# First stage reordered: Fourier tables early, broadcasts late, rows turned before the last modulation unit

## The reference

```python
c_act = silu(c)
mod = c_act @ w_ada + b_ada                    # 1024 x 6144: shift_m, scale_m, gate_m, shift_f, scale_f, gate_f
h = rms_norm(x, g_norm_mix) * (1 + scale_m) + shift_m
p = h @ w_in                                   # 512 + 5*1024 columns: u_f, v, b_g, c_g, ga, gb
y_a = fourier_mix(u_f) @ w_fourier             # a DFT over tokens and over 128 channels of each of 4 groups
y_b = (b_g * conv3(c_g * v)) @ w_conv_out
x = x + gate_m * ((sigmoid(ga) * y_a + sigmoid(gb) * y_b) @ w_o)
# then: 16 experts of width 2048 chosen by the tokens' scores, a second block with two kinds of
# sparse attention, and a third block (two layers) with four kinds of attention and a gated MLP
```

## Time and profile before

| | |
|---|---|
| median of 3 runs | 2204.26 us (2202.93 to 2204.53) |
| the profiled execution | 2204.55 us |
| its span, first to last instruction | 2202.8 us |
| TensorE (PE) busy | 1738.9 us, 79% |
| VectorE busy | 802.5 us, 36% |
| ScalarE busy | 637.9 us, 29% |
| granted TensorE clock, mean | 0.884 of 2.4 GHz |
| transferred | 613.54 MB, mean 279 GB/s |

### The profile page before, as it was taken

One profiled execution on the slowest core, in us unless ns is written; L12 is line 12 of the kernel. 1 busy time (PEld: TensorE's weight loads), 2 busy tenths in 40 slices (PEclk: granted clock), 3 DMA queues, 4 the chain that ended last, 5 costly groups with the idle time before them and its releaser, 6 DMA issues.

```text
span 2202.8 us, 32667 instructions
## 1 busy us (share of the span) xinstructions
PE 1738.9 (79%) x13392; PEld 1261.2 (57%) x13392; DVE 802.5 (36%) x1579; ACT 637.9 (29%) x1128; POOL 79.6 (4%) x133
## 2 busy tenths in 40 slices
PE   6999966565665666656555899879989998999998
PEld 3789921111121221112111799878879987989996
DVE  3364621111101111111100657665655545565553
ACT  2334310000000000000000456635644334654333
POOL 2000010000000000000000200100100000000000
PEclk8999977888878777787878899999989999989999
DMA  9886779999999999999999653316164544145540
GB/s 350 296 286 231 287 286 428 428 429 428 428 428 429 428 428 428 429 429 428 428 428 421 213 192 116 96 68 225 26 224 154 191 164 148 40 154 163 190 167 26
DMA packets 152998, 613.54 MB, mean 279 GB/s; under 512 B 8816, under 2 KB 62138, under 8 KB 128312
## 3 DMA queue, kind: packets, MB, share of 16 engines
q1 hardware_dynamic: 148928, 604.47, 69.7%
q0 software_dynamic: 3200, 7.14, 1.1%
q10 hardware_dynamic: 760, 0.39, 0.1%
HBM read 610.88 MB, written 5.03 MB: 280 GB/s over the span
## 4 chain that ended last, share of the span: by engine, by line
PE 51%; DMA 38%; DVE 5%; issue 3%; ACT 2%; DVEq 1%; POOL 1%; SPq 0%; ACTq 0%; POOLq 0%
PE psum L1393 49%; DMA ring<-in_w_down_e 18%; DMA ring<-in_w_up_e 18%; DVE ring_r L685 2%; PE psum L1475 1%; DMA ring<-in_w_in 1%; DMA x<-in_x 1%; PE psum L1721 1%; ACT arena L1046 0%; DVE arena L2271 0%; ACT ring_r L676 0%; DVEq L2265 0%; POOL stat L924 0%; DVE arena L2405 0%; POOL stat L927 0%
## 5 line engine op out<-in xcount | busy, mean ns | idle before, releaser
L1393 PE MATMUL psum<-ring,arena 128*32 128x512 f32 (+2 forms) x4314 | 534.3, 639 | 281.0 <-DMA ring<-in_w_up_e 129.5
L1393 PE MATMUL psum<-xR_r,ring_r 128*128 128x256 f32 x4416 | 561.4, 287 | 5.4 <-DVE xR_r L1931 3.4
L1393 PEld LDWEIGHTS psum<-xR_r,ring_r 128*128 128x128 f32 x4416 | 540.7, 193 | 16.7 <-issue 9.5
L1393 PEld LDWEIGHTS psum<-ring,arena 128*32 128x32 f32 x4314 | 153.7, 133 | 627.9 <-DMA ring<-in_w_up_e 209.6
L685 DVE TENSOR_TENSOR ring_r<-ring,ring_r 128x1024 fp32r<-128x1024 f32 (+2 forms) x332 | 377.7, 1173 | 255.1 <-ACT ring_r L676 254.7
L676 ACT CAST ring_r<-ring 128x1024 fp32r<-128x1024 f32 (+2 forms) x332 | 319.2, 1006 | 441.3 <-PE psum L1393 421.2
L1393 PE MATMUL psum<-arena 128*128 128x256 f32 (+7 forms) x1270 | 193.6, 387 | 26.4 <-DVE arena L2148 9.9
L2145 DVE TENSOR_TENSOR arena<-arena,psum 128x512 f32<-128x512 f32 x16 | 16.9, 1054 | 474.1 <-PE psum L1393 474.1
L1393 PE MATMUL psum<-ring_r,xR_r 128*128 128x256 f32 (+3 forms) x1344 | 176.5, 289 | 10.6 <-DVE xR_r L1909 6.1
L1393 PEld LDWEIGHTS psum<-ring_r,xR_r 128*128 128x128 f32 x1344 | 166.8, 195 | 14.2 <-issue 5.0
L1393 PE MATMUL psum<-ring_r,arena_r 128*128 128x512 f32 (+1 forms) x912 | 170.6, 349 | 2.1 <-DVE mt L2509 2.1
(11 more groups left out here) (242 smaller groups left out, 941.2 us busy)
## 6 DMA issues: line engine op xcount, KB each, us to landing
ring<-in_w_gate_e SPq DMA_DIRECT2D x64, 2048.0 KB, 25.9
ring<-in_w_down_e SPq DMA_DIRECT2D x63, 2048.0 KB, 26.4
ring<-in_w_up_e SPq DMA_DIRECT2D x62, 2048.0 KB, 24.8
ring<-in_w_in SPq DMA_DIRECT2D x30, 2048.0 KB, 12.3
ring<-in_w_ada SPq DMA_DIRECT2D x12, 2048.0 KB, 9.6
ring<-in_w_gate SPq DMA_DIRECT2D x22, 1024.0 KB, 5.5
ring<-in_w_up SPq DMA_DIRECT2D x22, 1024.0 KB, 8.5
ring<-in_w_down SPq DMA_DIRECT2D x10, 2048.0 KB, 7.8
```

Source lines behind the costliest of these rows:

```text
L1393: return nc.tensor.matmul(o, l, r, start=s, stop=e)
```

## The change

- SyncE asks for the two Fourier tables right behind `win0`, on a semaphore of their own (`in_dft`); the two gate broadcasts come behind `win3`, the router's loads, its bias and `g_final` behind `win5`.
- GpSimd's two replications wait until `uf0` is finished.
- The transposes `n1_0` to `n1_2` come ahead of the first step of `ada1`; `n1_3` comes behind its second step. The numbering of pieces, and with it the banks, changes: `uf0` (piece 8) now shares its bank with `n1_1` (4), `n1_3` (7) with `n1_0` (3).
- ScalarE writes the high part of the modulated rows (one activation with scale and bias, straight out of PSUM), and for `n1_1` and `n1_3` a full copy too; VectorE writes the full copy for `n1_0` and `n1_2`, and the low parts.
- `dfta` comes behind `v0`, `dftb` behind `v1`.
- In all blocks TensorE waits for the first low half of a chunk at a piece's beginning, for the second ahead of the second half of the contraction.

```diff
-PIECES = ([f"ada{u}" for u in ADA_FIRST] + names("n1_", 4) + names("uf", 2) + names("dfta", 4) + names("dftb", 2)
-          + with_ada(names("v", 4) + names("b", 4) + names("c", 4) + names("ga", 4) + names("gb", 4))
+PIECES = ([f"ada{u}" for u in ADA_FIRST[:3]] + names("n1_", 3) + [f"ada{ADA_FIRST[3]}", "n1_3"] + names("uf", 2)
+          + ["v0"] + names("dfta", 4) + with_ada(["v1"]) + names("dftb", 2)
+          + with_ada(names("v", 4)[2:] + names("b", 4) + names("c", 4) + names("ga", 4) + names("gb", 4))
...
+        moved = bT[:, 0:4, :].rearrange("p (a b) t -> p a b t", a=2)
...
                 if i == 0:
+                    sp.dma_start(dfts, a["c_dft"][:, 0:TT * 2 * T].rearrange("p (k n) -> p k n", k=TT)).then_inc(in_dft, 16)
+                    sp.dma_start(dftg, a["c_dft"][:, TT * 2 * T:].rearrange("p (k n) -> p k n", k=2)).then_inc(in_dft, 16)
+                if i == 3:
                     sp.dma_start(gate_m, a["b_ada"][:, 2 * D:3 * D].partition_broadcast(P).squeeze(1)).then_inc(in_b1, 16)
                     sp.dma_start(gate_f, a["b_ada"][:, 5 * D:6 * D].partition_broadcast(P).squeeze(1)).then_inc(in_b1, 16)
-                    sp.dma_start(dfts, a["c_dft"][:, 0:TT * 2 * T].rearrange("p (k n) -> p k n", k=TT)).then_inc(in_b1, 16)
-                    sp.dma_start(dftg, a["c_dft"][:, TT * 2 * T:].rearrange("p (k n) -> p k n", k=2)).then_inc(in_b1, 16)
+                if i == 5:
                     sp.wait_ge(consts_set, 6)
...
             pool.wait_ge(rel_na, 16 * 9)
+            pool.wait_ge(g_ready, AT["uf0"] + 1)
             pool.dma_start(na_rep.rearrange("r (q n) -> r q n", q=GRID_W),
...
+            def high_moved(h):
+
+                i = AT[f"n1_{h}"]
                 piece(act, i)
+                if h == 0:
+                    act.wait_ge(mod_set, 1)
+                if h % 2 == 0:
+                    act.wait_ge(n1_full, h // 2 + 1)
+                for full in (False, True)[:1 + h % 2]:
+                    for m in range(2):
+                        k = 2 * h + m
+                        d = moved[:, h // 2, m, :] if full else xR[:, 0, k, :]
+                        o = nc.scalar.activation(d, G(i)[:, m * T:m * T + T], ACT.Identity, bias=mod[:, k:k + 1],
+                                                 scale=Am[:, k:k + 1])
+                o.then_inc(n1_hi, 1)
+
+            high.half(0, 0)
+            high_moved(0)
+            high.half(0, 1)
+            for h in range(1, 4):
+                high_moved(h)
+            for i in range(2):
+                high.half(1, i)
...
+            def split_half(blk, name, l, i):
                 c = (C1AT, C2AT, C3AT)[blk][name]
-                pe.wait_ge(c_low[blk], (0 if l is None else l * (2 * len(CH3))) + 2 * (c + 1))
-                return chunk(blk, c)[1:]
+                pe.wait_ge(c_low[blk], (0 if l is None else l * (2 * len(CH3))) + (2 * c + i + 1))
+
+            def second_half(k, kt, blk, name, l):
+                if k == kt // 2:
+                    split_half(blk, name, l, 1)
...
             for p, u in enumerate(ADA_FIRST):
+                if p == 3:
+                    pe.wait_ge(n_xn, 1)
+                    for h in range(3):
+                        turn_first(h)
+                    mod_second(ADA_FIRST[2])
                 mod_first(u)
-                if p >= 1:
+                if 1 <= p < 3:
                     mod_second(ADA_FIRST[p - 1])
             mod_second(ADA_FIRST[-1])
+            turn_first(3)
...
+            def low_moved(h):
+                i = AT[f"n1_{h}"]
+                full = moved[:, h // 2, :, :] if h % 2 else temp(h // 2)
+                v.drain()
+                dve.wait_ge(n1_hi, h + 1)
+                v.tensor_tensor(xs[1][:, 2 * h:2 * h + 2, :], full, xs[0][:, 2 * h:2 * h + 2, :].bitcast(F32),
+                                ALU.subtract).then_inc(g_free[i % 4], 1)
...
+            full_moved(0)
+            low.half(0, 0)
+            low_moved(0)
+            low.half(0, 1)
+            full_moved(2)
+            for h in range(1, 4):
+                low_moved(h)
             for i in range(2):
-                low.half(0, i)
-            modulated(AT["n1_0"], Am, mod[:, 0:8])
-            low.ahead(-1)
+                low.half(1, i)
```

More of the change, by code:

```diff
@@ L1102, in _, with taken_rows @@
             high = High(act, 0)
-            high.ahead(-1)
-            for i in (AT["uf0"], AT["uf1"]):
-                high.ahead(C1AT[f"uf{i - AT['uf0']}"])
+            def high_moved(h):
+                i = AT[f"n1_{h}"]
                 piece(act, i)
-                h = i - AT["uf0"]
+                if h == 0:
[16 more added lines that the diff above has]
+                high.half(1, i)
+            def taken_rows(nm, dstT, h):
+                i = AT[f"{nm}{h}"]
+                piece(act, i)
+                nc.scalar.copy(dstT[:, 2 * h:2 * h + 2, :],
+                               G(i).rearrange("p (k t) -> p k t", k=2)).then_inc(g_free[i % 4], 1)
+            for h in range(2):
+                i = AT[f"uf{h}"]
+                piece(act, i)
                 nc.scalar.copy(uf[:, :, 256 * h:256 * h + 256],
                                G(i).rearrange("p (t n) -> p t n", t=TT)).then_inc(g_free[i % 4], 1)
+                high.ahead(C1AT[f"uf{h}"])
+            taken_rows("v", vT, 0)
+            high.ahead(C1AT["v0"])
             for g in range(4):
@@ L1114, in _ @@
             for nm, dstT in (("v", vT), ("b", bT)):
-                for h in range(4):
-                    i = AT[f"{nm}{h}"]
+                for h in range(nm == "v", 4):
                     high.ahead(C1AT[f"{nm}{h}"])
-                    piece(act, i)
-                    nc.scalar.copy(dstT[:, 2 * h:2 * h + 2, :],
-                                   G(i).rearrange("p (k t) -> p k t", k=2)).then_inc(g_free[i % 4], 1)
+                    taken_rows(nm, dstT, h)
                     if f"{nm}{h}" in ADA_AFTER:
@@ L1463, in cols3, with turn_first @@
                 return ready(o, l) if r == count - 1 else o
+            def turn_first(h):
+                i = AT[f"n1_{h}"]
+                bank_free(pe, i)
+                for m in range(2):
+                    for t in range(TT):
+                        k = 2 * h + m
+                        o = nc.tensor.transpose(G(i)[:, m * T + t * P:m * T + t * P + P], xn1[:, t, k * P:k * P + P], ident)
+                o.then_inc(g_ready, 1)
             def turn_x(first, src, l=None, normed=None, at=0):
@@ L1529, in _ @@
             xs = (xR[:, 0], xR[:, 1])
[L1530 to L1531 removed]
             for h in range(2):
[L1533 to L1550 removed]
+                rows3(AT[f"uf{h}"], 0, f"uf{h}", xs, first=[AT[f"n1_{j}"] for j in range(4)] if h == 0 else None)
             prior = None
@@ L1554, in _ @@
                     cols3(AT[f"{nm}{h}"], 0, f"{nm}{h}", xs)
+                    if f"{nm}{h}" == "v0":
+                        taken(pe, AT["uf0"], AT["uf1"])
+                        pe.wait_ge(in_dft, 16 * 2)
+                        for g in range(4):
+                            i = AT[f"dfta{g}"]
+                            bank_free(pe, i)
+                            for k in range(TT):
+                                o = mm(G(i), uf[:, k, g * P:g * P + P], dfts[:, k, :], k == 0, k == 1)
+                            o.then_inc(g_ready, 1)
                     if f"{nm}{h}" in ADA_AFTER:
@@ L1558, in _ @@
                         mod_second(ADA_AFTER[prior])
+                    if f"{nm}{h}" == "v1":
+                        for c_ in range(2):
+                            i = AT[f"dftb{c_}"]
+                            bank_free(pe, i)
+                            for m in range(2):
+                                g = 2 * c_ + m
+                                taken(pe, AT[f"dfta{g}"])
+                                for c in range(2):
+                                    o = mm(G(i)[:, m * T:m * T + T], dftg[:, c, :], Bcs[:, g, c * T:c * T + T], c == 0, c == 1)
+                            o.then_inc(g_ready, 1)
                     prior = f"{nm}{h}"
@@ L2005, in _ @@
                     low.ahead(C1AT[f"{nm}{h}"])
-            dve.wait_ge(in_b1, 16 * 4)
+                    if f"{nm}{h}" == "v1":
+                        for c in range(2):
+                            i = AT[f"dftb{c}"]
+                            piece(dve, i)
+                            parts(pair(G(i)), (fmR[:, 0], fmR[:, 1]), slice(2 * c, 2 * c + 2)).then_inc(g_free[i % 4], 1)
+            dve.wait_ge(in_b1, 16 * 2)
             gate_half(0)
```

57 lines of the change are left out of this document (19 added, 38 removed).

## The result

The changed kernel takes 2190.58 us (median of five, 2186.11 to 2193.42), beside 2204.53 us for the kernel before in the same set. The medians differ by 13.95 us, where 10.1 were forecast (2194.2). The ratio over the single executions is 0.9927 [0.9911, 0.9943], which is 16.1 us. Two further timed sets of both kernels give 0.9937 [0.9924, 0.9950] and 0.9921 [0.9906, 0.9936], and one single time is 2187.9 us; together about 16 us. The direction was right, and so were the places, but for some that were missing. The size was too small by 4 to 6 us.

A forecast was written before the change was run, and what follows sets the result against it. TensorE was taken as the chain from 64.46 us until the experts, which are DMA bound. Stage one -7.2 and half waits -3.0 took 10.2 off 2204.55; with the median 0.3 lower, 2194.2 us, range 2190 to 2199 (8 in 10).

The forecast's parts named there:

- the term of the half waits: All blocks: TensorE starting on a chunk's first half shortens its waits for low halves, -3.0 us, bounds 0 and -5.
- The term of stage one: Ahead of the experts: stall -5.3, Fourier products -2.25, their cut +0.3, together -7.2 us, bounds -4.6 and -8.4.
- The head: Start to end of `uf1`: vectors ready at 39.6 us, `uf0` starts at 45.8, `uf1` ends at 59.2 (58 to 61.5).
- my formula: End of `uf1` is 57.3 + 0.44 h us, h being how long the low clock stays, 3.1 to 4.5 us.
- The stall and the Fourier products: Behind `uf1`: `win1` lands near 42 us, ending the stall, -5.3 us; Fourier products at 2.4 GHz, -2.25, cut in two, +0.3.
- What is moved later: Replications, gate broadcasts and router loads cost nothing; `win3` lands at 79 us, needed at about 89, slack 10 us.
- the signs of being wrong: `uf0` starting after 47 us, a wait for `win3` near 89 us, or layer three as long as before.
- The rival of the collision: Replications collide with `win3`: 21.4 us on its way, landing at 81 us; slower by 0.2% only from 104; chance 0.04.
- the likeliest: Whole kernel: all terms count, 2194.2 us, own range 2191 to 2197; chance 0.55.
- only stage one counts: Rival: half waits only move a wait to the next VectorE result, 2197.1 us; chance 0.2.
- the stall stays: Rival: `win1` still lands after 58 us, set by something other than queue order, 2200 to 2203 us; chance 0.05.
- the head is later: Rival: slower ScalarE-VectorE hand-overs or clock rising only in 7 us, `uf1` ends at 62, 2197 to 2200 us; chance 0.13.

The follow-up runs named there:

- queue_only: The kernel before with the new order of requests alone, replications behind `uf0` included: 2203.56 us, 0.9986.
- old_queues: The changed kernel with broadcasts, tables, router loads and replications asked for as in the kernel before: 2200.83 us, 0.998.
- after_fourth: The changed kernel, unaltered, timed again beside another kernel on one chip: 2186.66 us, 0.9921 to the kernel before.
- reps_early: The changed kernel, but GpSimd's two replications go as soon as their sources are there, not behind `uf0`: 2197.14 us, 0.9964.
- half_only: The kernel before with the half waits alone, in all blocks: 2198.59 us, 0.9968.
- warm_whole: The changed kernel with whole waits everywhere, 22 unread small products in the head and 8 ahead of layer two's second branch product: 2189.85 us, 0.9925.
- whole_waits: The changed kernel, but a piece waits for both low halves again: 2192.56 us, 0.9945.
- before_warm: The kernel before with 12 unread small products in two idle places of TensorE's head: 2203.32 us, 0.9990.

## Why the size was off

The mechanisms of the sum held, and its size did not. The step that failed is the term of the half waits: -3.0 us, where the runs show 5.5 to 6.8 us, 5.6 of them idle time. The term of stage one, -7.2 us, was too small by 0.8 us on average over four traces (8.0), and its bounds by more.

- **The head**: right. The vectors, the start of `uf0` and the end of `uf1` came within 0.7 us. The 0.7 us are the low clock: it lasted 6.0 us from the start of `uf0` (45.63 to 51.67) and not 3.1 to 4.5, and with 6.0 my formula gives 59.9 ahead of its 0.2 for the first load. What was missing is the spread. The rule that I quoted from the Trainium skill ("TensorE: Matmul & The Clock Gate", section "What's actually happening"), that the moment at which the clock rises differs from run to run, bears far more than the 0.6 us that I gave it: the traces agree with it, for the low stretch ended anywhere from 47.4 to 51.7 us, and the start of `uf0` moved from 45.6 to 43.3 us. The step that failed here is "bounds -4.6 and -8.4": the start of `uf0` was taken for fixed, "1 us earlier" at best if the vectors come at 2.4 GHz, when it is 2.3, and -8.4 was passed by one trace in four.
- **The stall and the Fourier products**: right. Stage one came out at 6.9 us in the first trace of the changed kernel, where -7.2 was the sum. queue_only and old_queues show that it needs both the queue and the order of the pieces.
- **What is moved later**: "Cost nothing, slack 10 us" was wrong, though it cost nothing. `win3` needs 29.0 us beside the replications (26.1 to 32.4 in the four traces), not the 20 that my sum over all queues gives. In after_fourth it is asked for at 56.89 and needs the 32.4 us. There ScalarE does wait for it:

```profile
89.30 2.00 ACT L681 CAST ring_r<-ring 128x1024 fp32r<-128x1024 f32 x2 [11.02 <-DMA ring<-in_w_in]
```
```profile
ring<-in_w_in SPq DMA_DIRECT2D x1, 2048.0 KB, 32.4
```

  TensorE has no idle time behind it even there. A wait for `win3` near 89 us was among the signs of being wrong. The rival of the collision was named, the collision is real, and its price of 21.4 us was 5 to 11 too low. The rule that I quoted there (the Trainium skill, "DMA: Bandwidth & Descriptors", section "Queues, rings and completion order": an engine takes turns between queues) agrees in direction: from 61.2 to 89 us SyncE's queue moved 4.89 MB and GpSimd's 3.27 MB, and `win3` took 29.0 us, where three units that were asked for between 27 and 36 us, each with others of its queue ahead of it, took 16.8 to 20.7. The two gate broadcasts asked for right behind `win3` share that time; their part is not told apart. The delay also saved what I had not seen, `win2` (reps_early): a gain of its own, hidden in the term of the stall.
- **The half waits**: the term that was mis-sized. -3.0 us, with a bound at -5, measured 5.5 to 6.8 us. Most of it is idle time, as the steps in the traces show, and a further part is the clock:

| place | forecast | in the traces |
|---|---|---|
| convolution's output product, 228 us | 0 | 1.0 |
| three small waits in the second block | 0.3 (for four) | 1.5 |
| layer two | 1.3 | 1.2 |
| layer three, two passes | 1.4 | 1.9 |
| sum | 3.0 | 5.6 |

  The break at 228 us I did not count, since the wait there was put down to `issue`. The small waits, 0.18, 0.38 and 0.22 us in the rows, I took at less than their length, and each gave more. In layer two "the wait of 3.85 us shrinks by the second half of a small chunk, 0.65 us" held to 0.05 us, but the 72 products behind it were left at the low clock in my sum. They are 2.4 to 2.7 us shorter when the clock falls ahead of the wait, as in all four traces. Of this the layer kept 1.2 to 2.8 us (2.4 to 4.0 in all, less the 1.2 of idle time). I had worked out what the clock gives back for the Fourier products, and not for the same pattern 1350 us later. Why it falls ahead of the wait in 10 of 11 traces with half waits, half_only the exception, is not shown; in warm_whole, with whole waits, it did so too (the 24 products in 3.75 us).
- **The base**: my sum started from the quickest trace of the kernel before; the mean of three traces is 0.6 us behind it at `v2` and 0.9 us at the end. The last subtraction has a slip as well: 2194.35 less 0.3 is 2194.05, not 2194.2.
- **The sum** by the four traces of the changed kernel, on average and against the first of before: stage one 8.0, the break at 228 us 1.0, from there to 1416 us 1.9 (from 4.0 gained to 0.4 lost; the three small waits are 1.5 of it in every trace, for the rest I can't name a cause), layer two 3.4, what is behind it 2.2 (0.2 to 4.0): 16.5 us at the end. Behind layer two, kernels with whole waits throughout also move by anything from 0.3 us lost to 4.3 gained (whole_waits, before_warm), so only the two steps of 0.95 us there are shown to be the half waits'. The other two traces of before end 1.8 and 1.0 us behind the first. By their ratios the three timed sets give 16.1, 13.9 and 17.4 us of 2205.

The chances stood well (faster by over 0.2% at 0.88), and the median of the first set lies in the range by 0.6 us, outside the likeliest's own. That it lies inside is in part luck: by the ratio, 0.9927 of 2204.26, the time would be 2188.2 us, below the range; after_fourth, with 2186.66, and the single 2187.9 us lie below it too. Of the rivals, "only stage one counts" is refuted by half_only, "the stall stays" by the landing of `win1` at 44.5 us, "the head is later" by all four traces.

## What to carry to other kernels

List every place where the engine on the chain stands, those put down to `issue` too: the short ones here gave back their wait and 0.2 us more. Price a wait ahead of a long run of products twice: the idle time, and the clock behind it (2.4 to 2.7 us for 72 products here); and read a shorter wait against the start of what it waits for, since a slower product ahead of it shortens it too. When a transfer is moved out of one unit's way, write down the next units with request, rate and landing, for it will share the queues with one of them. And where TensorE idles a few us ahead of its main work for reasons of data, small products that nobody reads can pay: in the new order they brought stage one from 8.0 to 11.4 us, in the old one, where they ran at the low clock themselves and a late transfer stood behind, nothing.

## What the runs showed that I had not expected

- Products that nobody reads pay: 22 of them in some 8 us of idle time made stage one 3.4 us shorter on average, and the same within 0.3 us in each of six traces.
- Executions of one unchanged kernel differ by 2 to 13 us in one set (the changed kernel from 2183.44 to 2192.84, the kernel before from 2199.86 to 2212.72). Between traces of the changed kernel the distance arises in the head, where the moment of the clock differs, between 231 and 1416 us, where one loses 0.4 us and another gains 4.0, and behind layer two (0.2 to 4.0).
- A unit of 2 MB that takes 16.8 to 20.7 us behind others of its queue takes 26.1 to 32.4 us beside two replications of 3.9 MB from device memory to device memory and two small broadcasts, while the DMA engines were not full: 0.82 of their time and 285 GB/s from 60 to 90 us, in the changed kernel.
